# A decoder trunk on one core: output columns turned by products with diag(final_g), rows scaled on two engines

## The reference

```python
def rmsnorm(x, g):
    xf = x.astype(jnp.float32)
    y = xf * lax.rsqrt(jnp.mean(xf * xf, axis=-1, keepdims=True) + EPS)
    return (y * g.astype(jnp.float32)).astype(x.dtype)

def layer(x, c, ...):
    ...
    x = x + g2 * ((jax.nn.gelu(uc) * v) @ ffn_w_down)
    return x, h_last, new_lc, new_sc, new_fc

def run_trunk(x, ..., final_g):
    for l in range(DEPTH):
        x, h, lc, sc, fc = layer(x, ...)
    y = rmsnorm(x, final_g)
    return y, ...
```

## Time and profile before

| | us |
|---|---|
| median of 3 runs | 1337.21 |
| lowest and highest | 1336.83, 1337.5 |
| the profiled execution | 1338.02 |
| its span (first to last instruction) | 1336.4 |
| PE busy in it | 1308.4 (98%) |
| DVE busy | 711.2 (53%) |
| ACT busy | 489.1 (37%) |

### The profile page before, as it was taken

How to read it: one execution, slowest core, us unless ns; L and a number is a source line. 1 busy time by engine, 2 the same in 40 slices (tenths; PEclk the granted TensorE clock), 3 DMA queues, 4 the chain that set the end, 5 groups by cost and what they waited for, 6 DMA issues and landing times.

```text
span 1336.4 us, 23646 instructions
## 1 busy us (share of the span) xinstructions
PE 1308.4 (98%) x9715; PEld 1247.3 (93%) x9715; DVE 711.2 (53%) x1259; ACT 489.1 (37%) x647; POOL 47.6 (4%) x94
## 2 busy tenths in 40 slices
PE   5999999999999999999999999999999999999998
PEld 4788888899999999999999888999999999999997
DVE  4463863675444543554487186367544454354545
ACT  5424753453233222232344376245322222123231
POOL 0300000000000000000010000000000000000001
PEclk9999999999999999999999999999999999999999
DMA  9654655522222222222243565411222221222202
GB/s 300 211 173 175 220 190 189 190 72 72 97 93 78 94 71 87 85 72 94 66 142 99 185 212 174 150 64 64 80 84 94 91 94 65 94 73 85 94 32 97
DMA packets 115837, 157.10 MB, mean 118 GB/s; under 512 B 3543, under 2 KB 108984, under 8 KB 110645
## 3 DMA queue, kind: packets, MB, share of 16 engines
q1 hardware_dynamic: 108413, 112.55, 25.6%
q0 software_dynamic: 7168, 43.47, 9.5%
q10 hardware_dynamic: 184, 0.06, 0.0%
HBM read 153.08 MB, written 2.99 MB: 117 GB/s over the span
## 4 chain that ended last, share of the span: by engine, by line
PE 92%; DVE 4%; DMA 2%; ACT 1%; issue 1%; DVEq 0%; SPq 0%; POOLq 0%; ACTq 0%
PE ps L381 25%; PE ps L383 24%; PE ps L382 24%; PE ps L400 4%; PE ps L401 4%; PE ps L402 4%; PE ps L447 3%; DMA ada_w<-in_w_ada 2%; DVE w_lo L1018 1%; PE ps L529 1%; PE ps L624 1%; PE ps L458 1%; DVE norm_lo L1028 0%; DVE work L1086 0%; ACT w_hi L719 0%
## 5 line engine op out<-in xcount | busy, mean ns | idle before, releaser
L381 PE MATMUL ps<-norm_hi,w_hi 128*128 128x288 f32 x1792 | 533.1, 297 | 0.0
L382 PE MATMUL ps<-norm_lo,w_hi 128*128 128x288 f32 x1792 | 528.6, 295 | 0.0
L383 PE MATMUL ps<-norm_hi,w_lo 128*128 128x288 f32 x1792 | 526.8, 294 | 0.0
L381 PEld LDWEIGHTS ps<-norm_hi,w_hi 128*128 128x128 f32 x1792 | 335.8, 187 | 16.8 <-issue 15.9
L383 PEld LDWEIGHTS ps<-norm_hi,w_lo 128*128 128x128 f32 x1792 | 337.5, 188 | 0.0
L382 PEld LDWEIGHTS ps<-norm_lo,w_hi 128*128 128x128 f32 x1792 | 336.5, 188 | 0.0
L1018 DVE TENSOR_TENSOR w_lo<-w_raw,w_hi 128x2048 fp32r<-128x2048 f32 x91 | 208.4, 2290 | 87.6 <-ACT w_hi L719 87.5
L719 ACT ACTIVATE w_hi<-w_raw 128x2048 fp32r<-128x2048 f32 x91 | 173.8, 1910 | 156.7 <-PE ps L383 152.4
L381 PE MATMUL ps<-mid_hi,w_hi 128*128 128x288 f32 x704 | 209.3, 297 | 0.0
L382 PE MATMUL ps<-mid_lo,w_hi 128*128 128x288 f32 x704 | 207.7, 295 | 0.0
L383 PE MATMUL ps<-mid_hi,w_lo 128*128 128x288 f32 x704 | 207.0, 294 | 0.0
(11 more groups left out here) (212 smaller groups left out, 1376.3 us busy)
## 6 DMA issues: line engine op xcount, KB each, us to landing
w_raw<-in_ffn_w_up SPq DMA_DIRECT2D x44, 1024.0 KB, 5.0
ada_w<-in_w_ada POOLq DMA_DIRECT2D x40, 1024.0 KB, 5.2
w_raw<-in_w_in SPq DMA_DIRECT2D x20, 1024.0 KB, 5.5
w_raw<-in_ffn_w_down SPq DMA_DIRECT2D x16, 1024.0 KB, 5.2
ada_first<-in_w_ada SPq DMA_DIRECT2D x8, 1024.0 KB, 10.3
w_raw<-in_w_out SPq DMA_DIRECT2D x8, 1024.0 KB, 5.2
w_raw<-in_ffn_w_down SPq DMA_DIRECT2D x8, 768.0 KB, 4.4
work<-in_x_prompt SPq DMA_DIRECT2D x4, 512.0 KB, 6.9
```

Of the source, the lines that this page charges most:

```text
L381: T.matmul(out, WH[:, r, k, c:c + P], xh[:, k, h, :], start=start, stop=False)
L382: T.matmul(out, WH[:, r, k, c:c + P], xl[:, k, h, :], start=False, stop=False)
L383: last = T.matmul(out, WL[:, r, k, c:c + P], xh[:, k, h, :], start=False, stop=stop)
```

## The change

It does three things in the end of the kernel, and nothing elsewhere. A new tile FGD holds, for each channel block k, a 128x128 matrix with final_g on its diagonal. DVE makes it with one multiplication of FGB by the identity. The transposes of line 567 become ordinary products with FGD[k] as the moving operand, so that PSUM holds the turned columns already multiplied by final_g. The rows then need one factor only: ACT makes groups 0, 1, 2 and 4 and the second bank of group 5, DVE group 3 and the first bank of group 5, each with its own semaphore y_row[j]. And the last square of half 1 isn't added to ACC by DVE: PE makes two products for each group of tokens, one with ACC and one with the square itself, into the same PSUM column.

```diff
--- before.py
+++ after.py
@@ -121,6 +121,7 @@
         RS = [wk(4)[:, 0:HALF], wk(10)[:, 0:HALF]]
         NSR = WORK[:, 7 * PADW:7 * PADW + 6 * P].rearrange("p (i n) -> p i n", i=6)
         FGB = WORK[:, 0:D]
+        FGD = WORK[:, 5 * PADW:5 * PADW + D].rearrange("p (k n) -> p k n", k=KX)
         XROW = WORK[:, 0:6 * D].rearrange("p (a n) -> p a n", a=6)
         VROW = WORK[:, 6 * D:6 * D + 15 * P].rearrange("p (a n) -> p a n", a=15)
 
@@ -210,7 +211,9 @@
         c_cols, c_sig, c_ready, v_cols, v_ready = sem("c_cols"), sem("c_sig"), sem("c_ready"), sem("v_cols"), sem("v_ready")
         x_cols, lam_e = sem("x_cols"), sem("lam_e")
         x_copied, x_moved = sem("x_copied"), sem("x_moved")
-        fg_in, y_cols, y_rows, y_out = sem("fg_in"), sem("y_cols"), sem("y_rows"), sem("y_out")
+        fg_in, fg_ready, y_cols, y_out = sem("fg_in"), sem("fg_ready"), sem("y_cols"), sem("y_out")
+        y_row = [sem(f"y_row{j}") for j in range(6)]
+        last_square, rst_ready = sem("last_square"), sem("rst_ready")
         first_full = [sem(f"first_full{b}") for b in range(4)]
         first_used, first_rows, first_cols, first_mod = sem("first_used"), sem("first_rows"), sem("first_cols"), sem("first_mod")
         head_hi, head_lo, rs_copied, lam_ready = sem("head_hi"), sem("head_lo"), sem("rs_copied"), sem("lam_ready")
@@ -314,7 +317,7 @@
             ys = o["y_sample"].rearrange("b t n -> (b t) n")
             for j, y in enumerate(Y_ORDER):
                 i, h, t0, w = token_tiles()[y]
-                sp.wait_ge(y_rows, j + 1)
+                sp.wait_ge(y_row[j], 2 if j == 5 else 1)
                 dst = o["y_prompt"][0, i * P:(i + 1) * P, :] if i < 4 else ys[h * HS:(h + 1) * HS, :]
                 sp.dma_start(dst, YROW[i][0:w, :]).then_inc(y_out, 16)
             sp.wait_ge(y_out, 16 * 6)
@@ -564,7 +567,8 @@
 
                 i, h, t0, w = token_tiles()[Y_ORDER[j]]
                 for k in ks:
-                    last = T.transpose(PS[0:w, Y_BANK[j] + k // 4, (k % 4) * P:(k % 4 + 1) * P], X[:, k, h, t0:t0 + w], IDN[:])
+                    last = T.matmul(PS[0:w, Y_BANK[j] + k // 4, (k % 4) * P:(k % 4 + 1) * P], X[:, k, h, t0:t0 + w], FGD[:, k, :],
+                                    start=True, stop=True)
                 return last
 
             def y_tile(j):
@@ -684,24 +688,30 @@
                     pe.wait_ge(ns_read, L * 6)
                     norm_stats(L * 2 + 1, 0)
                 if (h, i, k) == (1, 1, KX - 1):
+                    pe.wait_ge(fg_ready, 1)
                     y_tile(0)
                 if (h, i, k) == (1, 2, KX // 2 - 1):
                     pe.wait_ge(std_ready, 4 * L + 1)
                     y_tile(1)
                 if (h, i, k) == (1, 2, KX - 1):
-                    pe.wait_ge(y_rows, 1)
+                    pe.wait_ge(y_row[0], 1)
                     y_tile(2)
 
             half_tiles_of_last_four((L - 1) * PL + T_DN[2] // 2 + 2, L * 2 + 1, after_last)
             pe.wait_ge(psum_free[0], read(L - 1, T_DN[2] + KX - 2))
             pe.wait_ge(x_ready, L * 24 - 1)
             y_part(3, range(KX - 1))
-            pe.wait_ge(y_rows, 2)
+            pe.wait_ge(y_row[1], 1)
             y_part(4, range(KX - 1))
-            norm_stats(L * 2 + 1, 1)
+            pe.wait_ge(last_square, 1)
+            for t0, w, c in half_tiles(1):
+                out = stat_bank(L * 2 + 1, 1)[0:w, c:c + 1]
+                T.matmul(out, acc_of(1)[:, t0:t0 + w], AVG[:, 0:1], start=True, stop=False)
+                last = T.matmul(out, halves(SQ[1])[:, 1, t0:t0 + w], AVG[:, 0:1], start=False, stop=True)
+            last.then_inc(stat_done, 1)
             for j in (3, 4):
                 y_part(j, [KX - 1]).then_inc(y_cols, 1)
-            pe.wait_ge(y_rows, 3)
+            pe.wait_ge(y_row[2], 1)
             y_tile(5)
 
 
@@ -986,9 +996,26 @@
             for i in range(4, 8):
                 square(L * 2 - 1, i)
             std(L * 2 + 1, 0)
-            for i in range(8, 12):
-                square(L * 2 - 1, i)
+
+            def y_scaled(j, banks):
+
+                i, h, t0, w = token_tiles()[Y_ORDER[j]]
+                act.wait_ge(y_cols, j + 1)
+                act.wait_ge(rst_ready, h + 1)
+                A(YROW[i][0:w].rearrange("p (b n) -> p b n", b=2)[:, banks], PS[0:w, Y_BANK[j]:Y_BANK[j] + 2, :][:, banks],
+                  ACT.Copy, scale=RST[0:w, 3 * h + t0 // P:3 * h + t0 // P + 1]).then_inc(y_row[j], 1)
+
+            square(L * 2 - 1, 8)
+            square(L * 2 - 1, 9)
+            y_scaled(0, slice(0, 2))
+            y_scaled(1, slice(0, 2))
+            square(L * 2 - 1, 10)
+            y_scaled(2, slice(0, 2))
+            act.wait_ge(x_ready, L * 24)
+            A(halves(SQ[1])[:, 1], X[:, KX - 1, 1], ACT.Square).then_inc(last_square, 1)
             std(L * 2 + 1, 1)
+            y_scaled(4, slice(0, 2))
+            y_scaled(5, slice(1, 2))
 
 
         @block.vector
@@ -1064,7 +1091,12 @@
 
                 c = 3 * h
                 dve.wait_ge(std_ready, m * 2 + (h - 1))
-                step(V.reciprocal(RST[:, c:c + 3], STD[:, c:c + 3]))
+                ins = V.reciprocal(RST[:, c:c + 3], STD[:, c:c + 3])
+                if m == 2 * L + 1:
+                    ins.then_inc(rst_ready, 1)
+                    dve.wait_ge(rst_ready, h + 1)
+                else:
+                    step(ins)
                 if m == 1:
                     V.tensor_tensor(DIAG0[:, c:c + 3], IDN[:].rearrange("p (u n) -> p u n", u=1).broadcast_to([P, 3, P]),
                                     RST[:, c:c + 3].rearrange("p (i u) -> p i u", u=1).broadcast_to([P, 3, P]),
@@ -1497,32 +1529,28 @@
                             end_and_norm(l, l * 2 + 1, T_DN[g], MOD_G2, (l, PL), (l + 1, 1), MOD_SH1)
                     made += K
 
-            def y_row(j):
+            def y_scaled(j, banks):
 
                 i, h, t0, w = token_tiles()[Y_ORDER[j]]
                 dve.wait_ge(y_cols, j + 1)
-                V.scalar_tensor_tensor(out=YROW[i][0:w].rearrange("p (b n) -> p b n", b=2),
-                                       in0=PS[0:w, Y_BANK[j]:Y_BANK[j] + 2, :],
-                                       scalar=RST[0:w, 3 * h + t0 // P:3 * h + t0 // P + 1],
-                                       in1=FGB[0:w].rearrange("p (b n) -> p b n", b=2),
-                                       op0=ALU.mult, op1=ALU.mult).then_inc(y_rows, 1)
+                V.tensor_scalar(YROW[i][0:w].rearrange("p (b n) -> p b n", b=2)[:, banks],
+                                PS[0:w, Y_BANK[j]:Y_BANK[j] + 2, :][:, banks],
+                                RST[0:w, 3 * h + t0 // P:3 * h + t0 // P + 1], None, ALU.mult).then_inc(y_row[j], 1)
 
             end = (L - 1, L * 2 - 1, T_DN[2], MOD_G2)
             end_of_first_half(*end)
             dve.wait_ge(fg_in, 16)
+            V.tensor_tensor(FGD, FGB.rearrange("p (k n) -> p k n", k=KX),
+                            IDN[:].rearrange("p (u n) -> p u n", u=1).broadcast_to([P, KX, P]), ALU.mult).then_inc(fg_ready, 1)
             sum_square(L * 2 - 1, 8)
             half_residual(*end, 9)
-            y_row(0)
             sum_square(L * 2 - 1, 9)
-            y_row(1)
             half_residual(*end, 10)
-            y_row(2)
             sum_square(L * 2 - 1, 10)
             half_residual(*end, 11)
-            sum_square(L * 2 - 1, 11)
             rstd(L * 2 + 1, 1)
-            for j in (3, 4, 5):
-                y_row(j)
+            y_scaled(3, slice(0, 2))
+            y_scaled(5, slice(0, 1))
 
 
 UP_STEPS = 6
```

## The result

| | before | changed |
|---|---|---|
| median, us (12 runs each) | 1336.96 | 1341.18 |
| lowest and highest | 1335.35, 1339.76 | 1339.39, 1343.2 |
| span of the profiled execution | 1336.4 | 1338.8 |

The changed kernel is slower: the medians differ by 4.2 us, and the ratio of the two is 1.0029 with a 95% interval of 1.0022 to 1.0037 (2.9 to 4.9 us). The forecast was 1341.4 in a range of 1339.8 to 1343.3.

The account below looks back on a forecast made before the run. PE, busy 98% of the span, was taken as the bound, with the DMA as last stage. Terms 2.7 + 1.0 + 0.65 − 0.06 gave +4.3 us (4.2 unrounded), span 1340.6, median 1341.4, range 1339.8 to 1343.3.

Parts of the forecast that it names:

- groups 0 to 2 in PE's stream: Inside half 1's stream on PE, 24 products replace 24 transposes, all on the path: +2.7 us.
- groups 3, 4 ahead of the statistics: Behind the last tile, 14 products take 3.1 us where transposes took 1.5, so the statistics start later: +1.0 us.
- the statistics: PE's statistics of half 1 have 12 records instead of 6, lasting 1.4 us, before 0.76: +0.65 us.
- The price of a product: On PE, a float32 product is two records of 0.110 us, 0.220 in all; a transpose is one of 0.109.
- The saved sum: DVE's dropped sum of the last square, 0.46 us, is worth nothing because PE still has products to do.
- the last rows on two engines: At the end, groups 4 and 5 shared with ACT are ready 1.3 us sooner, but beside the DMA: worth 0.
- The last transfers: At the end, three output transfers of 1.18 MB take 4.9 us from group 3's ready rows: start, transfer and landing.
- Diag(final_g): On DVE, 1.22 us, ready at 1316.8 before PE wants it at about 1317.5: 0, with 0.7 us to spare.
- A: Rival on PE: a product costs one transpose, being one instruction like it; +0.15 us, 1337.4; chance 0.10.
- B: Rival at the end: DVE's three rows, not the DMA, are the last stage, so 1.3 us is saved; 1340.1; chance 0.08.
- C: Rival on PE: a record cannot hide its weight load, so a product costs four transposes; +12.4 us, 1349.6; chance 0.05.
- D: Rival: diag(final_g) or a row group on ACT comes late and stops PE; 1342.4 with 1 us late; chance 0.05.

Follow-up runs that it names:

- e1: Kernel before with only its 48 transposes made float32 products with the identity: tail 36.8 us against 32.95 before, ratio 1.0045.
- e2: Changed kernel with transposes by the identity in place of the products, rows lacking final_g: tail 33.0 us, ratio 1.0; repeated, tail 33.0.
- e3: Kernel before with only DVE's last sum dropped and the last square of half 1 added by the statistics products: tail 33.0 us, ratio 1.0007.
- e4: Changed kernel with groups 3, 4 and 5 all made by DVE, one after another: tail 37.3 us against the changed kernel's 37.4, ratio to before 1.0036.
- e5: Changed kernel with groups 3, 4 and 5 each made in halves by DVE and ACT: tail 36.85 us against 37.4, ratio to before 1.0028.
- e7: Changed kernel with e5's rows, transposes kept, final_g multiplied into X by ACT before they turn it: tail 32.8 us, ratio to before 0.9997.
- e8: e7 without PE's wait for x_ready ahead of group 3's transposes: tail 32.8 us, ratio to before 0.9998.
- e6: Changed kernel with the statistics moved ahead of group 4's products: tail 36.4 us against 37.4, median 1341.1, ratio to before 1.0029.

## Why the prediction was right

The five terms, each the difference of two points of the timelines:

| term | forecast, us | measured, us | from |
|---|---|---|---|
| groups 0 to 2 in PE's stream | +2.7 | +3.05 | first record behind the last tile: 26.26 us into the tail against 23.21 |
| groups 3, 4 ahead of the statistics | +1.0 | +1.0 | 3.12 behind that record, before 2.11 |
| the statistics | +0.65 | +0.4 | 1.16 long, before 0.76 |
| from there to group 3's rows | −0.06 | 0 | 1.96, before 1.95 |
| from there to the end | 0 | 0 | 4.9, before 4.9 |
| sum | +4.3 | +4.45 | |

The mechanism of each term is the one that the runs show. The closeness of the sum is in part luck: the first term was 0.35 us too low and the third 0.25 too high.

**The price of a product** was right in its mechanism and near in its size: two records each, (1.95 − 0.27)/15 = 0.112 us apart, where I took 0.110 (0.107, the lower price of the prediction, stands in no row). For the two groups of prompt tokens in the stream this is the whole account. Group 1 holds PE for 1.70 us (1319.00 to 1320.70) where its transposes took 0.79, which is 0.91 more, and 16 × 0.112 − 8 × 0.109 = 0.92; group 0 gives 0.92. What I missed is the group of 32 sample tokens, which the same sum prices like the others. Its transposes cost what all transposes cost: in the kernel before they begin at 1322.58, 0.13 us behind the last L402, and hold PE for 0.79 us:

```profile
1322.45 0.29 PE L402 MATMUL ps<-mid_hi,w_lo 128*128 128x288 f32 x1
...
1323.37 0.38 PE L400 MATMUL ps<-mid_hi,w_hi 128*128 128x288 f32 x1
```

Its products do not. They begin 0.22 us behind the last L405 (1322.26 to 1322.48), where group 1's begin 0.13 behind it (1318.87 to 1319.00), and they hold PE for 1.88 us (to 1324.36) instead of 1.70. That is 0.09 + 1.09 = 1.18 us more than the transposes, some 0.27 above a prompt group. The three groups give 0.92 + 0.91 + 1.18 = 3.0 of the measured 3.05. The extra comes at both ends, where products of 32 tokens meet those of 128 columns; why is not shown. It isn't the rows on ACT, since e1 has the same step with the rows on DVE (its 16 records start at 1323.34, 0.22 us behind the product before them), nor PE's wait ahead of this group, which the kernel before has as well. e1 shows that the products alone make the loss, e2 that without them nothing is lost.

**The statistics** were overpriced. I took 0.69 us for the six records of half 0, 0.114 each, by taking the stream's first product to lie 0.13 us ahead of its second, at 1313.65. Its own row says otherwise:

```profile
1313.55 0.40 PE L400 MATMUL ps<-mid_hi,w_hi 128*128 128x288 f32 x1
```

The six took 0.59 us (1312.96 to 1313.55); 0.1 us is a step behind that product, 0.23 to the second one at 1313.78, which is no part of the stretch from the first record of the statistics to their last. Here the twelve take 1.10 us to the next group's first record (1330.78 to 1331.88), 0.09 each on average but not evenly: those of 128 tokens stand 0.112 apart (1330.92 to 1331.14 for two), those of 32 closer.

**The saved sum, and the last rows on two engines as the change has them,** were worth nothing, each for the reason given: the sum was hidden behind PE's products (e1 starts the statistics at the same point with the sum; e3 shows that with transposes, too, its removal is only exchanged for records), the rows behind the transfers (e2, e4). Two engines pay only on group 3, which the end follows (e5). The prices of single rows were a little low: 1.28 us for DVE and 1.11 for ACT, against 1.22 and 1.02 of plain copies. Neither is on the path beyond group 3's.

**The last transfers** were read a little short: their bytes fill 20 slices of 0.15 us, 3.0 us until 1335.35 and not 2.7 until 1335.1, and the end is 1.05 us behind them and not 1.3. The 4.9 us, which is all that the sum uses, are the same.

**Diag(final_g)** took 1.22 us and was ready in time; PE has no gap ahead of its first use. The rows of groups 0 to 2 on ACT delayed no square.

**The rivals.** A (a product is one record) falls by the 96 records. B (the end follows the last rows) falls by e2, e4 and e5. C (four transposes' worth) falls by the distance 0.112: a product is 0.224 us and a transpose 0.109, a factor of two and not of four. D left no stop on PE.

## What to carry to other kernels

Price a replacement on the bound engine by the distance of its records, and count the records first: an instruction that reads like the old one may be two. Price each shape by rows of its own: the group of 32 tokens cost 0.27 us more than the others. If the transposed data need a factor per column, put it on the data while that index is still the partition, where an idle engine does it in one operand, and leave the transpose exact; here that cost nothing that a timed run could tell (e7, e8), and gained nothing over the old kernel either. And before the last rows are sped up, look at what the last transfers do: when they run without a gap, only the first of those rows counts, as long as the later ones come before its bytes are through (in e6 they did not).

## What the runs showed of the hardware

- A 128 by 128 float32 product is two records of 0.112 us at a granted clock of 1.00, so 0.224 against 0.109 for a transpose. Each has its own weight load of 0.19 us, which the distance of 0.112 shows to be hidden behind other records.
- Between three-part products, eight such products with 128 stationary columns hold PE for 1.70 us and begin 0.13 us behind the product before them; with 32 stationary columns 1.88 and 0.22. Transposes make no such difference: 0.79 and 0.13 us for eight with either.
- DVE scaling 128x1024 out of PSUM by one number per partition takes 1.284 us, as long as with a second tensor operand, 1.282. The same on ACT takes 1.113, and 0.68 for half of the columns.
- The three output transfers (1.18 MB) need 4.9 us from the first ready row to the end, some 0.9 to the first byte, 3.0 to 3.2 in which packets start and 0.9 to 1.05 behind that, in every kernel in which the first group leads.
